# Four small reorderings in a one-core kernel of two transformer blocks: factors in four places, rows ahead of maxima, a score sum ahead of a split, a shift over 128 rows

## The reference

```python
# first block
mod = silu(c) @ w_ada + b_ada                    # six rows of 1024: sh1, sc1, g1, sh2, sc2, g2
h = rms_norm(x) * (1 + sc1) + sh1
qa, ka, va, qb, kb, vb, gl = split(h @ w_in)     # q and k normed and rotated
oa = 12 heads of dilated window attention, 3 groups merged by their log-denominators
ob = 8 heads of (softmax(q1 k1^T) - lam * softmax(q2 k2^T)) v, then rms_norm
x = x + g1 * ((sigmoid(gl)[0] * (oa @ w_proj_a) + sigmoid(gl)[1] * (ob @ w_proj_b)) @ w_out)
h2 = rms_norm(x) * (1 + sc2) + sh2
x = x + g2 * peer_ffn(h2)                        # top 16 of 16384 experts for each of 8 heads
# second block
x = x + conv and gated recurrence mixer(x);  x = x + cross attention(x, mem)
x = x + mixture of experts(x)                    # 16 experts; then a last rms_norm
```

## Time and profile before

| | |
|---|---|
| median of 3 runs | 1869.84 us (1866.72 to 1872.03) |
| profiled execution, its own time | 1871.05 us |
| its span from first to last instruction | 1869.3 us |
| mean granted TensorE clock | 0.991 |
| PE busy | 1827.0 us, 98% of the span |
| DVE, ACT, POOL busy | 1371.7, 912.0, 77.6 us |

### The profile page before, as it was taken

How to read it: one execution, slowest core, us unless ns; L and a number is a source line. 1 busy time by engine, 2 the same in 40 slices (tenths; PEclk the granted TensorE clock), 3 DMA queues, 4 the chain that set the end, 5 groups by cost and what they waited for, 6 DMA issues and landing times.

```text
span 1869.3 us, 24560 instructions
## 1 busy us (share of the span) xinstructions
PE 1827.0 (98%) x9392; PEld 1530.4 (82%) x9392; DVE 1371.7 (73%) x1903; ACT 912.0 (49%) x1013; POOL 77.6 (4%) x101
## 2 busy tenths in 40 slices
PE   8999999999999999999999999999999999999998
PEld 4778766888899877888888888889988888888886
DVE  5679588669998665666666666667875688888897
ACT  2553465311334444444444444456645467667675
POOL 0000000100000431110000000000000000000000
PEclk9999899999999999999999999999999999999999
DMA  7655365434446785666555555555343589898884
GB/s 310 247 181 201 113 225 192 158 125 147 163 153 229 248 275 188 212 210 222 182 200 180 196 185 191 190 184 191 143 143 127 219 312 360 319 354 325 340 342 183
DMA packets 61697, 404.94 MB, mean 217 GB/s; under 512 B 8129, under 2 KB 8417, under 8 KB 15281
## 3 DMA queue, kind: packets, MB, share of 16 engines
q1 hardware_dynamic: 51904, 371.22, 54.2%
q0 software_dynamic: 5968, 20.82, 3.9%
q10 hardware_dynamic: 3746, 11.83, 1.9%
HBM read 391.25 MB, written 12.58 MB: 216 GB/s over the span
## 4 chain that ended last, share of the span: by engine, by line
PE 84%; DVE 7%; DMA 3%; ACT 3%; issue 1%; DVEq 0%; ACTq 0%; SPq 0%
PE ps L2339 18%; PE ps L2341 17%; PE ps L2340 17%; PE ps L2733 9%; PE ps L2451 7%; PE ps L2735 4%; PE ps L2761 3%; DVE wlo L1241 2%; DMA raw<-in_stream_dram 2%; ACT whi L693 2%; DMA BIG<-in_stream_dram 1%; PE ps L2942 1%; PE ps L2461 1%; PE ps L2563 1%; PE ps L2584 1%
## 5 line engine op out<-in xcount | busy, mean ns | idle before, releaser
L1241 DVE TENSOR_TENSOR wlo<-raw,whi 128x2048 fp32r<-128x2048 f32 x179 | 410.2, 2292 | 201.3 <-ACT whi L693 201.1
L693 ACT ACTIVATE whi<-raw 128x2048 fp32r<-128x2048 f32 x179 | 343.0, 1916 | 375.7 <-PE ps L2341 190.3
L2733 PE MATMUL ps<-tboth,whi 128*128 128x512 f32 x736 | 259.8, 398 | 0.0
L2339 PE MATMUL ps<-whi,phi 128*128 128x512 f32 x608 | 238.9, 393 | 6.2 <-DVE plo L1832 6.2
L2341 PE MATMUL ps<-whi,plo 128*128 128x512 f32 x608 | 237.4, 391 | 0.0
L2340 PE MATMUL ps<-wlo,phi 128*128 128x512 f32 x608 | 237.4, 391 | 0.0
L2339 PE MATMUL ps<-whi,tboth 128*128 128x512 f32 (+1 forms) x576 | 226.7, 394 | 7.0 <-DVE wlo L1241 4.2
L2341 PE MATMUL ps<-whi,tboth 128*128 128x512 f32 (+1 forms) x576 | 223.1, 387 | 0.0
L2340 PE MATMUL ps<-wlo,tboth 128*128 128x512 f32 (+1 forms) x576 | 223.0, 387 | 0.0
L2735 PE MATMUL ps<-tboth,wlo 128*128 128x256 f32 x644 | 181.0, 281 | 0.0
L2451 PE MATMUL ps<-h2T,raw 128*128 128x256 f32 x768 | 172.4, 380 | 0.0
(11 more groups left out here) (426 smaller groups left out, 3074.7 us busy)
## 6 DMA issues: line engine op xcount, KB each, us to landing
raw<-in_stream_dram SPq DMA_DIRECT2D x259, 1024.0 KB, 4.8
BIG<-in_stream_dram SPq DMA_DIRECT2D x84, 1024.0 KB, 6.6
BIG<-g_spill POOLq DMA_DIRECT2D x64, 128.0 KB, 4.8
BIG<-in_stream_dram SPq DMA_DIRECT2D x2, 2048.0 KB, 16.3
spare<-in_stream_dram SPq DMA_DIRECT2D x4, 1024.0 KB, 7.2
g_spill<-H ACTq DMA_DIRECT2D x4, 1024.0 KB, 4.8
g_spill<-MOD ACTq DMA_DIRECT2D x4, 1024.0 KB, 4.8
MID<-in_gains_dram POOLq DMA_DIRECT2D x7, 512.0 KB, 4.0
```

Source lines behind the costliest of these rows:

```text
L693: nc.scalar.activation(whi[:, u % 2, :], raw_of(u), ACT.Copy).then_inc(unit_hi, 1)
L1241: nc.vector.tensor_tensor(wlo[:, u % 2, :], raw_of(u), whi[:, u % 2, :].bitcast(f32), ALU.subtract).then_inc(unit_split, 1)
L2339: nc.tensor.matmul(out, ahi, bhi, start=start, stop=False)
L2733: last = nc.tensor.matmul(out, whi[:, s, cols], both, start=c == 0, stop=c == DC - 1)
```

## The change

Four places are touched, and SM grows so that `b_rec` can have 16 columns.

```diff
-        SM = sb("SM", [P, 280])
+        SM = sb("SM", [P, 288])
...
-        b_max, b_sum, b_rec = col(8), col(8), col(8)
+        b_max, b_sum, b_rec = col(8), col(8), col(16)
...
             def b_rows(h):
...
-                    got, r = ps[:, 5, t * P:(t + 1) * P], b_rec[:, 4 * (h % 2) + t:4 * (h % 2) + t + 1]
+                    got, r = ps[:, 5, t * P:(t + 1) * P], b_rec[:, 4 * (h % 4) + t:4 * (h % 4) + t + 1]
...
                 ada_sum(DC + i)
                 if i + 2 < n_a:
                     a_mask(i + 2)
-                else:
-                    b_maxima(i + 2 - n_a)
                 if i:
                     a_rows(i - 1)
+                if i + 2 >= n_a:
+                    b_maxima(i + 2 - n_a)
             a_rows(n_a - 1)
...
             def b_weights(h):
-                r = b_rec[:, 4 * b:4 * b + 4]
-                if h >= 2:
-                    dve.wait_ge(b_out, 2 * TT * (h - 1))
+                r = b_rec[:, 4 * (h % 4):4 * (h % 4) + 4]
+                if h >= 4:
+                    dve.wait_ge(b_out, 2 * TT * (h - 3))
...
             lo(at_u(EARLY + 1))
+            summed(EARLY)
             lo(at_v(EARLY))
-            summed(EARLY)
             gated(EARLY)
...
-                    nc.tensor.matmul(ps[:, tr_bank(t, k), :].rearrange("p (c t) -> p c t", c=4), shift_rows[0:DC, :],
-                                     ident[0:DC, chunks].unsqueeze(2).broadcast_to([DC, 4, P]), start=True, stop=False)
+                    nc.tensor.matmul(ps[:, tr_bank(t, k), :].rearrange("p (c t) -> p c t", c=4), shift_rows,
+                                     ident[:, chunks].unsqueeze(2).broadcast_to([P, 4, P]), start=True, stop=False)
```

## The result

The changed kernel takes 1858.05 us (median of 7 runs, 1854.10 to 1861.49); seven runs of the kernel before, the three of the table above among them, gave 1866.72. The ratio is 0.9933, 95% interval 0.9911 to 0.9955. Two more sets gave 0.9946 (0.9924 to 0.9967) and 0.9952 (0.9936 to 0.9968), so the gain is 8.7 to 10.9 us where 4.75 were forecast. The profiled execution took 1854.1.

A forecast was written before the change was run, and what follows sets the result against it. PE was taken as the bound (84% of the chain), so edits count where PE waits or is half-clocked. 1.25 + 0.1 + 3.3 + 0.1 = 4.75 us, from the median 1869.84, gave 1865.1 us; 8-in-10 range 1861.5 to 1869.0.

The forecast's parts named there:

- part 2: Second attention, factors in four places: 0.1 us gained; 1.4 us at its end taken as hidden beside the first projection's load.
- Part 1: Seam of the two attentions, rows ahead of maxima: `b_transposes(1)` starts 1.25 us earlier, with the clock staying at 1.00.
- part 3: Late experts, score sum ahead of the split: 1.83 us off the chain plus 1.5 by the clock, 3.3 us gained.
- Part 4: Shift matmuls over 128 rows instead of 8: 0.1 us gained, bounds 0.19 either way.
- the end of the attention counts: Rival at the first projection: its unit lands earlier, part 2's 1.4 us are not hidden; 6.2 us gained, 1863.7; chance 0.15.
- a rival on the slower side: BIG moves 32 bytes; slower loads or reads there cost the second block's experts, 1876.5 us at 3%; chance 0.05.
- the 256-byte rule: Loads into BIG: a row not starting on a multiple of 256 bytes costs one transaction more; they gain some 3%.

The follow-up runs named there:

- h4: Kernel before with the normalised rows ahead of the next head's maxima and the first late score sum ahead of the split: 1865.69 us (its kernel before 1870.02).
- g2: Changed kernel with the second attention's factors in two places again, SM kept at 288 columns: 1859.86 us (its kernel before 1869.07).
- f1: Kernel before with only the shift's matmuls reading 128 rows instead of 8: 1868.25 us (its kernel before 1869.27).
- e1: Kernel before with only SM widened from 280 to 288 columns, so BIG starts 32 bytes later: 1867.36 us (its kernel before 1868.85).

## Why the prediction was wrong

The forecast was 1865.1, with 1861.5 as its lower end. Of the 7.0 us to the result, 3.1 are the starting point: it went from 1869.84, and the kernel before gave 1866.72 in the first comparison. That was a low draw of seven runs and no error of the forecast, as the five later sets gave 1868.85 to 1871.11. The rest is the gain: 4.75 forecast, 8.7, 10.9 and 9.05 measured, 10.5 between the means of the 120 and the 19 runs. So the failed steps are those that were put at next to nothing: the clock at the shift, BIG's place, and the wait of part 2.

- **Part 1 (1.25 us) and part 3 (3.3 us): right.** In the trace `b_transposes(1)` gained 1.20 and `values_of(18)` 1.96, PE's idle stretch there is 0.85 (forecast 0.94), both falls are gone, and h4 gives 4.5 for the pair. By chance more than by reasoning: the clock's full price was taken from one profile that had both falls, while they come in two or three of five executions; the pair's clock still summed to 2.2 against 1.9.
- **Part 4 (0.1 us): the mechanism was missed.** The step asked how long the eight matmuls take, and there it was right: 3.44 us in place of 3.63, its upper bound. It did not ask what eight rows do to the clock. The profile of before could not show it, since it is the one 8-row profile of six without a fall there. Worth about 2 us.
- **Part 2 (0.1 us; 1.4 "lie beside the load"): too small.** The load that was to hide them took 8.11 us in the one profile that the step read and 6.6 to 6.8 in seven of the 13 with four places. The end of the attention came 1.9 us earlier, not 1.4. The rival "the end of the attention counts" named the mechanism, but for the reason that it gave (the load starts earlier) no run speaks; its 1.4 were 1.3, in g2's profile and at the same clock.
- **BIG's move (0, or a rival on the slower side): the wrong sign.** The rival looked at the big loads into BIG and at PE's reads, and applied the 256-byte rule to those big loads alone. These did not change: the 8192-byte packets from 1500 to 1800 us, most of which go to BIG, took 336 to 340 ns in the mean with BIG off a multiple of 128 and 335 to 342 on one. The small loads from `g_spill` to the same tile, on POOL's queue, were not in the sum. The stand of 1.3 us at 696.70 goes with them, a row that was in front of me and was used only as a measure of idle time. PE's reads got faster by 0.4%, not slower. Worth 1.8 us alone, 2.8 to 3.2 when undone.

Sum of what was measured: 4.5 (h4) + 1.8 (f1) + 1.3 (g2) + 1.8 (e1) = 9.4. The changed kernel's mean clock is .0027 above that of before, 4.5 us; at the same clock it gains 5.9, where the steps taken singly give 5.4. Together that is 10.4 against 9.4, within the spread of the single steps.

## What to carry to other kernels

An edit that moves a tile is an edit of every transfer and every read of the tiles behind it: list them by the size of their runs, and look first at the small ones, even on a queue with 4% of the DMA time. An edit of the shape of a matmul has to be asked for the clock, not only for its duration. And one profile shows one draw, of the clock and of a load's length: price a fall by how often it comes, and before calling a wait hidden, ask whether the load that hides it is always that long.

## What the runs showed of the hardware

- In or right behind matmuls over 8 of 128 rows, 3.6 us of them with PE busy throughout, the clock halved in five profiles of six; over 64 rows (one profile) and 128 (thirteen) in none.
- The router's 32 matmuls of 20 columns, with PE busy, had half clock behind or in them in all 20 profiles, and 1.1 us of 256-column matmuls in their middle did not change it (one profile).
- 4096-byte packets made of 128-byte runs, 760 to 845 us: 204 to 205 ns in the mean with the target on a multiple of 128 bytes, 274 to 280 off it.
- One 1 MB load at the same place, beside the same work: 6.6 to 6.8 us in seven profiles of 13, 7.7 to 8.0 in six.
- Matmuls reading 2 KB rows of `whi_b` and `wlo_b` (L2339, L2341, L2340): 400, 395 and 394 ns with them at a multiple of 256, 395, 390 and 390 at 128 past one, 400, 398 and 396 at 32 short of one. Why is open.
